# A two-layer decoder trunk on one core: first pw1 chunk by token tiles, pw2 bias laid out as 16x128

## The reference, cut to what matters

```python
def conformer_conv_layer(x, norm_pre, w_pw1, b_pw1, w_dw, b_dw, ln_g, ln_b,
                         w_pw2, b_pw2, norm_post):
    h = rms_norm(x, norm_pre)
    p = jnp.einsum('bsd,de->bse', h, w_pw1) + b_pw1
    g = p[..., :D_C] * jax.nn.sigmoid(p[..., D_C:])
    conv = lax.conv_general_dilated(
        g, w_dw[:, None, :], window_strides=(1,), padding=[(CONV_K - 1, 0)],
        dimension_numbers=('NWC', 'WIO', 'NWC'), feature_group_count=D_C) + b_dw
    c = jax.nn.silu(layer_norm(conv, ln_g, ln_b))
    y = jnp.einsum('bse,ed->bsd', c, w_pw2) + b_pw2
    return x + rms_norm(y, norm_post)
```

## Time and profile before

| | |
|---|---|
| Median of 3 runs | 2026.07 us (2025.24 to 2029.02) |
| Profiled execution | 2025.78 us, span 2023.9 us |
| PE busy | 1999.4 us, 99% |
| DVE, ACT, POOL busy | 1188.9, 982.9, 199.1 us |
| Chain that ended last | PE 88%, DVE 9%, ACT 1% |
| Granted TensorE clock, mean | 0.996 of full |

### The profile page before, as it was taken

One profiled execution on the slowest core, in us unless ns is written; L12 is line 12 of the kernel. 1 busy time (PEld: TensorE's weight loads), 2 busy tenths in 40 slices (PEclk: granted clock), 3 DMA queues, 4 the chain that ended last, 5 costly groups with the idle time before them and its releaser, 6 DMA issues.

```text
span 2023.9 us, 27880 instructions
## 1 busy us (share of the span) xinstructions
PE 1999.4 (99%) x9852; PEld 1697.5 (84%) x9852; DVE 1188.9 (59%) x1496; ACT 982.9 (49%) x1147; POOL 199.1 (10%) x123
## 2 busy tenths in 40 slices
PE   9999999999999999999999999999999999999998
PEld 7898888888888888888899977888888888888886
DVE  6755565555555554444699975655555555554444
ACT  6544464545455443433744465454444444443433
POOL 1000000000000000000589830000000000000000
PEclk9999999999999999999999989999999999999999
DMA  9545566766666666555355525576666676665554
GB/s 345 203 146 189 175 213 225 220 221 212 216 210 224 219 220 196 188 196 195 125 195 178 171 96 196 170 242 214 212 215 221 218 218 216 216 211 196 191 193 146
DMA packets 137534, 407.58 MB, mean 201 GB/s; under 512 B 15282, under 2 KB 38322, under 8 KB 136946
## 3 DMA queue, kind: packets, MB, share of 16 engines
q1 hardware_dynamic: 135364, 396.84, 60.0%
q0 software_dynamic: 2096, 9.70, 1.3%
HBM read 392.84 MB, written 13.63 MB: 201 GB/s over the span
## 4 chain that ended last, share of the span: by engine, by line
PE 88%; DVE 9%; ACT 1%; issue 1%; DMA 0%; POOL 0%; SPq 0%; DVEq 0%; ACTq 0%
PE acc L1267 83%; DVE acc L1181 7%; PE acc L1278 1%; PE acc L1280 1%; PE acc L1279 1%; PE acc L1495 1%; DMA raw<-in_units 0%; ACT w_hi L559 0%; PE acc L1319 0%; DVE gated L1168 0%; DVE conv L1186 0%; DVE conv L1181 0%; DVE w_lo L888 0%; ACT junk L569 0%; DVE conv L1219 0%
## 5 line engine op out<-in xcount | busy, mean ns | idle before, releaser
L890 DVE SCALAR_TENSOR_TENSOR w_lo<-raw,vecs,w_hi 128x1024 fp32r<-128x1024 f32 x400 | 511.7, 1283 | 443.1 <-ACT w_hi L559 442.8
L559 ACT ACTIVATE w_hi<-raw,vecs 128x1024 fp32r<-128x1024 f32 x400 | 460.3, 1152 | 523.0 <-PE acc L1267 485.2
L559 ACT ACTIVATE w_hi<-raw 128x1024 fp32r<-128x1024 f32 x304 | 321.2, 1059 | 397.1 <-PE acc L1267 351.7
L1267 PE MATMUL acc<-w_hi,xT_hi 128*128 128x512 f32 x1536 | 475.0, 390 | 4.9 <-DVE w_lo L890 2.5
L888 DVE TENSOR_TENSOR w_lo<-raw,w_hi 128x1024 fp32r<-128x1024 f32 x236 | 288.8, 1225 | 320.9 <-ACT w_hi L559 320.9
L1267 PE MATMUL acc<-w_lo,xT_hi 128*128 128x512 f32 x1536 | 473.1, 389 | 0.0
L1267 PE MATMUL acc<-w_hi,xT_lo 128*128 128x512 f32 x1536 | 473.0, 389 | 0.0
L1267 PEld LDWEIGHTS acc<-w_hi,xT_hi 128*128 128x128 f32 x1536 | 287.1, 188 | 67.3 <-issue 7.0
L1267 PEld LDWEIGHTS acc<-w_lo,xT_hi 128*128 128x128 f32 x1536 | 288.4, 188 | 60.1
L1267 PEld LDWEIGHTS acc<-w_hi,xT_lo 128*128 128x128 f32 x1536 | 288.4, 188 | 59.9
L1267 PE MATMUL acc<-w_hi,hT_lo 128*128 128x512 f32 x704 | 217.5, 389 | 0.0
(11 more groups left out here) (162 smaller groups left out, 1424.9 us busy)
## 6 DMA issues: line engine op xcount, KB each, us to landing
raw<-in_units SPq DMA_DIRECT2D x704, 512.0 KB, 4.1
hid_turned_blocks<-tok SPq DMA_DIRECT2D x44, 256.0 KB, 2.7
tok<-hid_turned_blocks SPq DMA_DIRECT2D x176, 64.0 KB, 2.7
gpost<-in_post POOLq DMA_DIRECT2D x4, 1024.0 KB, 5.3
x<-in_x POOLq DMA_DIRECT2D x4, 512.0 KB, 11.5
c_raw<-in_units POOLq DMA_DIRECT2D x4, 512.0 KB, 7.9
out<-x SPq DMA_DIRECT2D x8, 256.0 KB, 2.8
xT_raw<-in_xT SPq DMA_DIRECT2D x3, 512.0 KB, 7.8
```

What stands on the lines that cost most here:

```text
L559: nc.scalar.activation(w_hi[:, s, :], raw[:, s, :], ACT.Copy, scale=scale).then_inc(hi_ready, 1)
L890: ins = nc.vector.scalar_tensor_tensor(w_lo[:, s, :], raw[:, s, :], vecs[:, gain:gain + 1], w_hi[:, s, :], ALU.mult, ALU.subtract)
L1267: last = mm(acc[:, 4 * par + 2 * t + h, :], xs, ws[:, s, h * BANK:(h + 1) * BANK], start=start and ws is w_hi and xs is xh, stop=stop and ...
```

## The change

Chunk 0 of pw1 is computed with the other operand stationary: for each token tile, `xT_hi`/`xT_lo` of that tile are stationary and 256 weight columns are streamed, so the result has tokens on partitions. It is computed in two parts. Tile 0's part follows tile 0's turn; tile 1's turn stands inside it, ahead of block `TURN_AT` = 12. ACT copies each tile's result out of PSUM (`keep_chunk`) and PE transposes it back (`turn_chunk`, two 128x128 transposes for a tile) into bank 0, where the gate and the glu find it as before. The order on ACT and POOL changes too, two of the four squares of tile 0's x go to DVE, and half of tile 0's `lo_xc` moves ahead of tile 1's mean. The pw2 bias is loaded as 16x128, split there on 16 partitions, and two SBUF-to-SBUF DMAs place the parts into a `bias_rows` of two rows, between the loads of chunks 2 and 3. Left out below are the declarations of semaphores.

```diff
@@ -48,6 +48,7 @@
 RING = 4
 LAST = CCH - 1
 PE_WARM = 8
+TURN_AT = 12
 
 
 Q_V = 0
...
@@ -104,15 +105,15 @@
 
 def y_square(e, t, c):
 
-    at = 2 * t + c if c < 2 else 2 + c + t * (6 if e == 1 else 2)
-    return 8 + 16 * e + at
+    at = 2 * t + c if c < 2 else 2 + c + t * (4 if e == 1 else 2)
+    return 8 + 16 * e + at - (2 if e > 1 else 0)
 
 
 def x_square(b, t, c):
 
     if b == 0:
         return 4 * t + c
-    return 8 + 16 * (b - 1) + (6 * (t + 1) + c if b == 2 else 8 + 4 * t + c)
+    return 8 + 16 * (b - 1) + (6 + c if b == 2 and t == 0 else 10 + c if b == 2 else 8 + 4 * t + c) - (2 if b > 2 else 0)
 
 
 def by_tile_halves(t, c):
...
@@ -207,8 +208,11 @@
             conv_sum = mrow("conv_sum", [P, 2, SEQ])
             sq_sum = mrow("sq_sum", [P, 2, SEQ])
             diag = mrow("diag", [P, 2, SEQ])
-            bias_rows = mrow("bias_rows", [2 * 32, D], F32R)
-            ones_r = mrow("ones_r", [2 * 32, P], F32R)
+            bias_rows = mrow("bias_rows", [2, D], F32R)
+            ones_r = mrow("ones_r", [2, P], F32R)
+            bias_in = mrow("bias_in", [KT, P])
+            bias_hi = mrow("bias_hi", [KT, P], F32R)
+            bias_lo = mrow("bias_lo", [KT, P], F32R)
             taps = mb("taps", [P, KT, TAPS])
             gated = mb("gated", [P, RING, PAD + SEQ])
             sig = mb("sig", [P, RING, SEQ])
...
@@ -431,9 +438,13 @@
             load_quads(Q_F0 + Q_FF + 3, Q_POOL0 + 1, lo_ready, lo_count)
             sp.wait_ge(x_turned, 16)
             sp.dma_start(taps[:], d_taps).then_inc(taps_landed, 16)
-            for row in (0, 32):
-                sp.dma_start(tok[row:row + 1, :], d_bpw2[0:1, :]).then_inc(bpw2_landed, 16)
-            load_quads(Q_POOL0 + 1, Q_POOL1 + 1, lo_ready_pool, lo_pool_count)
+            sp.dma_start(bias_in[:], d_bpw2[0].rearrange("(k n) -> k n", n=P)).then_inc(bpw2_landed, 16)
+            load_quads(Q_POOL0 + 1, Q_POOL0 + 3, lo_ready_pool, lo_pool_count)
+            sp.wait_ge(bias_hi_ready, 1)
+            sp.dma_start(bias_rows[0:1, :].bitcast(F32).rearrange("p (k n) -> p k n", n=P), bias_hi[:].bitcast(F32)).then_inc(bias_placed, 16)
+            sp.wait_ge(bias_lo_ready, 1)
+            sp.dma_start(bias_rows[1:2, :].bitcast(F32).rearrange("p (k n) -> p k n", n=P), bias_lo[:].bitcast(F32)).then_inc(bias_placed, 16)
+            load_quads(Q_POOL0 + 3, Q_POOL1 + 1, lo_ready_pool, lo_pool_count)
             load_quads(Q_POOL1 + 1, Q_F1 + 4, lo_ready, lambda q, s: lo_count(q, s, True))
             load_ffn(1, Q_F1)
             load_quads(Q_F1 + Q_FF + 3, Q_END, lo_ready, lambda q, s: lo_count(q, s, True))
...
@@ -475,8 +486,8 @@
                     inv_root(*x_[0])
                     inv_root(*y[1])
                     split(Q_PW1, 1)
+                    split(Q_PW1, 2)
                     inv_root(*x_[1])
-                    split(Q_PW1, 2)
                     split(Q_PW1, 3)
                 else:
                     for root in y if e == 3 else y + x_:
...
@@ -754,33 +765,41 @@
 
             square_y(1, 1, 0, (2, 3))
             split(Q_PW1, 0)
-            square_x(2, 0, range(4))
+            square_x(2, 0, (0, 1))
+            split(Q_PW1, 1)
             square_y(1, 1, 1, (2, 3))
-            split(Q_PW1, 1)
             spread_rs(2, 0)
+            split(Q_PW1, 2)
+            hi_xc(0, range(4))
             for c in range(4):
                 square_x(2, 1, (c,))
-                if c:
-                    hi_xc(0, (2 * c - 2, 2 * c - 1))
-            hi_xc(0, range(6, 12))
+                if c < 3:
+                    hi_xc(0, (2 * c + 4, 2 * c + 5))
+            split(Q_PW1, 3)
+            hi_xc(0, range(10, 12))
             spread_rs(2, 1)
             hi_xc(0, range(12, 16))
-            hi_xc(1, range(8))
-            split(Q_PW1, 2)
-            hi_xc(1, range(8, 16))
-            split(Q_PW1, 3)
+            hi_xc(1, range(16))
 
             def split_bias():
 
-                act.wait_ge(bpw2_landed, 32)
-                act.wait_ge(bias_cleared, 1)
-                for row in (0, 32):
-                    nc.scalar.activation(bias_rows[row:row + 1, :], tok[row:row + 1, :], ACT.Copy).then_inc(bias_hi_ready, 1)
+                act.wait_ge(bpw2_landed, 16)
+                nc.scalar.activation(bias_hi[:], bias_in[:], ACT.Copy).then_inc(bias_hi_ready, 1)
                 act.wait_ge(consts_set, 2)
-                nc.scalar.activation(ones_r[:], ones[0:64, :], ACT.Copy).then_inc(bias_hi_ready, 1)
+                nc.scalar.activation(ones_r[:], ones[0:2, :], ACT.Copy).then_inc(bias_hi_ready, 1)
+
+            def keep_chunk(t):
+                if t == 0:
+                    act.wait_ge(first_chunk_ready, 1)
+                else:
+                    act.wait_ge(units_used, used_count(Q_PW1, 3))
+                nc.scalar.activation(sig[:, 2 + t, :], acc[:, 4 * t, 0:SEQ], ACT.Copy).then_inc(first_chunk_kept, 1)
 
             def gate(n):
-                act.wait_ge(units_used, used_count(Q_PW1 + n, 3))
+                if n:
+                    act.wait_ge(units_used, used_count(Q_PW1 + n, 3))
+                else:
+                    act.wait_ge(first_chunk_turned, 2)
                 if n >= RING:
                     act.wait_ge(glu_ready, n - RING + 1)
                 nc.scalar.activation(sig[:, n % RING, :], acc[:, n % RING, SEQ:2 * SEQ], ACT.Sigmoid,
...
@@ -803,10 +822,12 @@
                 nc.scalar.activation(sq[:, p % 2], conv[:, 2 * p:2 * p + 2, :], ACT.Square).then_inc(sq_ready, 1)
 
             nc.scalar.activation(warm[:], pow_exp[:], ACT.Sigmoid)
+            keep_chunk(0)
             split(Q_PW1 + 1, 0)
             split_bias()
             split(Q_PW1 + 1, 1)
             split(Q_PW1 + 1, 2)
+            keep_chunk(1)
             for n in range(LAST):
                 gate(n)
                 split(Q_PW1 + n + 1, 3)
...
@@ -1144,19 +1165,24 @@
             mean_square(y_sums, y_var, 0, y_square(1, 0, 3) + 1, y_var_ready)
             gain_y(1, 1, 0, (3,))
             add_y(1, 1, 0, range(4))
-            mean_square(x_sums, x_var, 0, x_square(2, 0, 3) + 1, x_var_ready)
+            for c in (2, 3):
+                xs = x[:, 0, c * BANK:(c + 1) * BANK]
+                dve.wait_ge(x_ready, added(2, 0, c))
+                last = nc.vector.scalar_tensor_tensor(tok[:, DA:DA + BANK], xs, 1.0, xs, ALU.mult, ALU.mult,
+                                                      accum_out=x_sums[:, 0, c:c + 1])
+                after(last)
+            mean_square(x_sums, x_var, 0, x_square(2, 0, 1) + 1, x_var_ready)
             gain_y(1, 1, 1, (2,))
             mean_square(y_sums, y_var, 1, y_square(1, 1, 3) + 1, y_var_ready)
             gain_y(1, 1, 1, (3,))
             add_y(1, 1, 1, range(4))
+            lo_xc(0, range(8))
             mean_square(x_sums, x_var, 1, x_square(2, 1, 3) + 1, x_var_ready)
-            lo_xc(0, range(16))
+            lo_xc(0, range(8, 16))
             lo_xc(1, range(16))
 
-            nc.vector.memset(bias_rows[:].bitcast(F32), 0.0).then_inc(bias_cleared, 1)
-            dve.wait_ge(bias_hi_ready, 3)
-            nc.vector.tensor_tensor(bias_rows[32:33, :], tok[32:33, :], bias_rows[32:33, :],
-                                    ALU.subtract).then_inc(bias_lo_ready, 1)
+            dve.wait_ge(bias_hi_ready, 2)
+            nc.vector.tensor_tensor(bias_lo[:], bias_in[:], bias_hi[:], ALU.subtract).then_inc(bias_lo_ready, 1)
 
             dve.wait_ge(consts_set, 3)
             dve.wait_ge(taps_landed, 16)
...
@@ -1468,8 +1494,32 @@
             ffn(0, Q_F0, 1, 0, 1)
 
 
+            turn_x(2, 1, 0, range(4))
             for t in range(T):
-                turn_x(2, 1, t, range(4))
+                for k in range(KT):
+                    u, ws = k // 4, slice((k % 4) * SEQ, (k % 4 + 1) * SEQ)
+                    if t == 0 and k % 4 == 0:
+                        pe.wait_ge(lo_ready_pool, lo_pool_count(Q_PW1, u))
+                    if t == 0 and k == TURN_AT:
+                        turn_x(2, 1, 1, range(4))
+                    pe.wait_ge(xc_lo_ready, conv_parted(t, k if t else max(k, 3)))
+                    out, ts = acc[:, 4 * t, 0:SEQ], slice(t * P, (t + 1) * P)
+                    mm(out, xT_hi[:, k, ts], w_hi[:, u, ws], start=k == 0, stop=False)
+                    mm(out, xT_hi[:, k, ts], w_lo[:, u, ws], start=False, stop=False)
+                    last = mm(out, xT_lo[:, k, ts], w_hi[:, u, ws], start=False, stop=k == KT - 1)
+                    if t == T - 1 and k % 4 == 3:
+                        last.then_inc(units_used, 1)
+                if t == 0:
+                    last.then_inc(first_chunk_ready, 1)
+
+            def turn_chunk(t):
+                pe.wait_ge(first_chunk_kept, t + 1)
+                for half in range(2):
+                    last = nc.tensor.transpose(acc[:, 0, half * SEQ + t * P:half * SEQ + (t + 1) * P],
+                                               sig[:, 2 + t, half * P:(half + 1) * P], ident[:])
```

(12 more changed lines are left out.)

5 lines of the change are left out of this document (4 added, 1 removed).

## The result

The changed kernel takes 2030.81 us, the median of 18 runs (2028.88 to 2033.59); the kernel before took 2027.62 us in the 18 runs beside them (2025.24 to 2030.2). The ratio is 1.0015 with a 95% interval of 1.0009 to 1.0021. By the medians that is 3.2 us slower, by the ratio 3.0 (1.8 to 4.3): under the 0.2% mark, though the interval reaches just past it. The forecast was +1.4 us and no change that counts, with 8 in 10 between 2024.2 and 2030.8. The profiled execution took 2030.41 us.

A forecast was written before the change was run, and what follows sets the result against it. DVE was taken to bound the pw1 stage, which moves with chunk 0's first tap; later weights of chunk 1 and added copy waits put that 1.4 us later: 2027.4 us from a median of 2026.07, 8 in 10 between 2024.2 and 2030.8.

The forecast's parts named there:

- What bounds: In the pw1 stage DVE sets the pace; the whole stage moves by as much as chunk 0's first tap.
- the sign that the prediction names for a lead taken for too large: In the changed profile: if DVE waits ahead of glu(1), PE was the limit and its lead was smaller than taken.
- Tile 0's scale: Two squares go from ACT to DVE: diagonal at 974.25 in place of 974.55, PE's turn 0.44 us later.
- Tile 1's turn: PE turns tile 1 at 985.15, released by POOL's low part of weight unit 3, 3.4 us later than before.
- Issue 990.0, landing 994.2: SyncE's first weight load of chunk 1 is issued at 990.0 and lands at 994.2, 3 us later than before.
- Loads that land together: Rival: chunk 1's four loads land close together near 996 to 998, +2.7 us; loads or clock alone 0.18, both 0.13.
- The sum: First tap 1.4 us later: profiled execution 2025.78 + 1.4 = 2027.2; from the median 2026.07, 2027.4.
- The clock's rival: Rival: the clock falls in PE's 1.2 us pause before chunk 1, +2.1 us; loads or clock alone 0.18, both 0.13.
- The early half pays: Rival, faster: chunk 0's early half brings the taps 1.1 or 1.8 us sooner if weights don't limit; chance 0.09.
- the floor of the gain: Fast end of the 8 in 10 range, 2024.2; taps up to 1.8 us sooner if weights were no limit.
- worth nothing now: DVE's 2.28 us of bias and its clearing vanish, but DVE then waits for the weights' chain: no gain.
- Two small operations, 0.4 us: ACT's 3.83 us of bias work becomes two small operations costed at 0.4 us, inside its wait for part 1.

The follow-up runs named there:

- e_after_again: The changed kernel once more without an edit, for a second profile and time: 2028.31 us.
- e_space: The changed kernel, but SyncE asks for weight parts 2 and 3 of chunk 1 only when part 0 has landed: 2029.87 us, ratio 1.0003.
- e_turn8: The changed kernel with TURN_AT 8 in place of 12, tile 1's turn four blocks sooner: 2028.34 us, ratio 0.9995.
- e_early: The changed kernel with SyncE waiting for 9 turned pieces instead of 16 before chunk 1's weights: 2027.25 us, ratio 0.9992.
- e_early_warm: e_early plus eight dummy 128x128 matmuls on PE ahead of tile 0's turn: 2027.92 us, ratio 0.9997.
- e_bias_only: The kernel before with the bias part of the change alone, chunk 0 as it was: 2027.46 us, ratio 0.999.
- e_bias_warm: e_bias_only plus eight dummy 128x128 matmuls on PE ahead of tile 0's turn: 2027.67 us, ratio 0.9991.
- e_chunk_only: The changed kernel with the old bias (two 1x2048 rows on ACT, 1x2048 on DVE): 2033.31 us, ratio 1.0023.
- e_k64: The changed kernel with 64 rows, 62 of them cleared, for the bias matmuls in place of two: 2030.64 us, ratio 1.0009.

## Why the prediction was off, point by point

**What bounds.** Right for the profile of the result: the stage moved by what the first tap moved (2.2 us there, 2.05 at glu(15)), DVE decided behind it, glu(1) came straight behind the taps. In e_after_again PE's lead was too small: DVE waited 0.59 us ahead of glu(1), the sign that the prediction names for a lead taken for too large.

**Tile 0's scale.** A few tenths too low. The two squares on DVE, which I had at 0.68 us:

```profile
971.57 1.12 DVE L1171 SCALAR_TENSOR_TENSOR tok<-x 128x512 f32<-128x512 f32 x1
972.62 0.08 DVE L1171 DVE_READ_ACCUMULATOR tok<-x 128x1 f32 x1
972.74 0.69 DVE L1171 SCALAR_TENSOR_TENSOR tok<-x 128x512 f32<-128x512 f32 x1
973.35 0.08 DVE L1171 DVE_READ_ACCUMULATOR tok<-x 128x1 f32 x1
973.47 0.16 DVE L929 TENSOR_REDUCE x_var<-x_sums 128x1 f32<-128x4 f32 x1
```

The operation by itself is the 0.69 that I had (the first spans 1.12 as it starts under the operation ahead of it), but behind each stands an instruction of its own that reads the accumulator, and from the end of the updates at 971.66 to the reduction at 973.47 the pair takes 1.8 us, where I had 1.4. The Trainium skill (VectorE: DVE Perf Modes, section on two Vector instructions with no wait between them) calls such an operation two instructions, the main one and an accumulator read; the trace agrees, and the "few tenths" more that I had worked out from it were the better sum. The diagonal was 2.28 us behind the last FFN matmul instead of 1.91 and the turn 2.73 instead of 2.36; nothing behind it paid, since the turn of tile 1 waits for other work. The slow first turn of 5.47 us that I had kept did not come in this profile (3.84) and did in the next; tile 1's turn was at +12.56 and +12.55.

**Tile 1's turn.** The moment was right, +12.56 for a forecast of +12.81; the releaser that I named was not: PE goes on straight behind the block ahead of it and shows no wait, since POOL's low part of unit 3 was done at 984.66, just before the 984.75 of the turn. From there to the first load's issue 4.99 us for 4.83.

**"Issue 990.0, landing 994.2": the step that failed.** I took 4.2 us from the earlier trace rows, a load with one neighbour, for a load with three. It landed in 5.6: 1.4 us of error, and everything behind it came later by it. This is some two thirds of the way to the rival "Loads that land together", which had the first part at 996 where the sum had 994.2; it came at 995.35. The rival was right that the first load pays for those behind it, not that the parts land close together, and I gave it too little: it was priced as all or nothing. The row that I set against it, 4.2 us with one load behind, did not have the case in it. e_space gives the size (4.3 with two under way, 5.6 with four), e_turn8 limits it (3.9 with four).

**The rate between the loads: an error the other way.** I spaced them 1.77 us by the 296 GB/s of the earlier trace rows; they came 1.2 us apart, so ACT's second copy waited less, and from PE's start of chunk 1 to the sigmoid it was 1.23 us in place of 1.70: 0.47 us back. The window's mean holds stretches in which SyncE waited for POOL before it asked for more; it was a rate of demand and not of the queue. With four loads queued the changed kernel moved 375 GB/s in 992 to 994, at a DMA share of 0.99 where the earlier trace rows had 0.87. The Trainium skill (DMA: Bandwidth & Descriptors, section on the anatomy of one DMA) fits 2.0 us plus the bytes at 436 GB/s to one DMA of GpSimd's queue, which for 512 KB gives an estimate of 3.2 us, 1.2 of it for the bytes. The trace, of SyncE's queue, agrees with the 1.2 us as the distance between queued loads and with the 3.2 us for the first load of e_early; no figure of the page gives the 5.6.

**The sum.** By steps, in us: the turn of tile 1 -0.25, turn to issue +0.16, landing +1.4, ACT and POOL to PE's chunk 1 -0.10 (a slip of my adding: 994.2 + 1.14 + 2.41 is 997.75 and not 997.85), from there to the sigmoid -0.47: +0.74, and the tap was measured at 30.30 for 29.51, +0.79. The place gave +2.2 instead of +1.4.

**The clock's rival.** PE's pause ahead of chunk 1 was 2.98 us instead of 1.2. In the profile of the result the clock stayed up and chunk 1 ended ahead of DVE; in e_after_again it fell, late enough to leave the transposes alone but not the end of chunk 1, which came behind DVE's need and cost 0.65 us at the last gate. I had chunk 1 "still ahead of DVE" in that case, from a start 1.2 us earlier. The late landing lengthens this pause, so as far as four profiles tell the loads' rival makes the clock's more likely.

**The rest of +3.2 us.** 2.05 us of it are at the last gate in one profile, 2.70 in the other. The runs show that some 2.5 us more or less stand in the tail by chance, so that the profile's 4.4 is the 2.05 and a long tail set against a short one. The last microsecond of the medians (the interval reaches down to 1.8) can be the clock behind the pause ahead of chunk 1 or long tails that are more frequent in the changed kernel; which was not settled, as two profiles of it can't tell. I had written that nothing changes behind glu(1), and had no term for this spread. The median before was also 1.6 us higher over 18 runs than the 2026.07 of the three I built on; without that 2030.81 would lie inside the range and not at its end. (2026.07 + 1.4 is 2027.5, where the prediction has 2027.4.)

**The early half pays, and what the bias gives.** I had written that the taps could start 1.1 us before now, or 1.8 with the clock up, if the weights were no limit. e_early came 0.71 sooner and e_early_warm, with the clock up, 1.05: the floor of the gain was sound. That DVE's bias work is "worth nothing now" I had right for the sum, but e_bias_only and e_bias_warm reach the same moment with the bias part alone: by these profiles all of that gain is the bias part's, none the early half's. And e_chunk_only shows that the bias part was not worth nothing in the new order; without it the tap was 2.6 us later.

**"Two small operations, 0.4 us."** Right: ACT's two took 0.39 together. But DVE's 2.28 us did not vanish. Its subtraction of 16x128 took 2.14 us, hardly less than the 2.28 of the 1x2048 one in the earlier trace rows, though each partition has a sixteenth of the elements. It lies in DVE's wait of 5.58 and 1.75 us, so it cost nothing. POOL's rows beside it, first of the kernel before, then of the changed one, show where the time goes:

```profile
997.38 3.54 POOL L465 TENSOR_TENSOR w_lo<-raw,w_hi 128x1024 fp32r<-128x1024 f32 x1 [2.62 <-ACT w_hi L559]
```

```profile
996.54 2.35 POOL L476 TENSOR_TENSOR w_lo<-raw,w_hi 128x1024 fp32r<-128x1024 f32 x1 [11.71 <-ACT w_hi L570]
```

In the changed kernel POOL's low part starts 0.35 us ahead of DVE's subtraction and ends at 998.89, the subtraction at 999.03. In all eleven profiles with the 16x128 subtraction it starts 0.34 to 0.36 us behind such a low part and takes 2.14 to 2.21 us. In the kernel before DVE is first: its subtraction ends at 998.66, and POOL's low part, begun at 997.38, takes 3.54 us instead of 2.4 and ends 2.26 behind it; e_chunk_only repeats this (3.53). So the operation that starts second seems to get nowhere until the first is done. No run was made to test this.

## What to carry to other kernels

When a step moves to a later place, look for everything that waits for its last piece on other engines' queues: here one wait of SyncE's for all sixteen turned pieces made a reordering of TensorE's work cost 3 us, and asking for nine took it back. A landing time read from a transfer with one neighbour need not hold for the first of four asked for at once, and a mean rate over a window that contains waits is no rate of the queue. Before a difference of 1 to 3 us between two profiles is put down to a change, profile the same kernel twice.

## What the hardware did that I had not expected

- The granted clock falls to 0.50 (1.2 GHz) while PE is busy for all of a window, in a run of matmuls with one column (5.68 us for 32 of them, 3.66 at full clock), and in some executions of a kernel it falls only behind them. The same holds behind a pause of 2.27 to 2.35 us: the next turn took 5.4 to 5.5 us in six profiles and 3.84 in five, once each in the changed kernel.
- The first of four 512 KB loads asked for within 2 us landed in 5.6, 5.6, 5.2, 4.8 and 3.9 us in five profiles (changed, again, e_k64, e_chunk_only, e_turn8), one with a single neighbour 0.6 us behind in 3.2 to 4.4. In the first four the others followed some 1.2 us apart.
- A DVE subtraction of 16x128 from fp32 into fp32r took 2.14 us where POOL's subtraction of 128x1024 had started 0.35 us ahead of it, and POOL's took 3.54 us instead of 2.4 where DVE's 1x2048 one was ahead.
